# Expert input matrices laid out by halves of the input, with a stationary router and rearranged additions behind the experts

## The reference

```
h2  = modulate(x, norm2_g, sh2, sc2)                  # 256 x 1024
gp  = softmax(h2 @ w_rg + b_rg)                       # 4 groups
el  = h2 @ w_re + b_re                                # 32 experts, 8 a group
g   = top1(gp); e0, e1 = top2(softmax(el[g]))         # two experts for each token
moe = sum over the two: weight * ((silu(h2 @ w1[e]) * (h2 @ w3[e])) @ w2[e])
x   = x + g2 * moe
x   = rms_norm(x, norm_f_g)                           # then the second block's own norm, and q, k, v
```

## Time and profile before

| | |
|---|---|
| median of 3 runs | 1377.7 us (1375.81 to 1378.25) |
| the profiled execution's own time | 1377.22 us |
| its span | 1375.4 us |
| mean granted TensorE clock | 0.944 |
| busy: PE, DVE, ACT | 1153.6, 611.5, 540.8 us |
| HBM read | 394.97 MB |
| chain that ended last | PE 61%, DMA 20%, DVE 10%, ACT 7%, issue 2% |
| loads of expert matrices | 52 into the five extra slots, 44 into the ring |

### The profile page before, as it was taken

How to read it: one execution, slowest core, us unless ns; L and a number is a source line. 1 busy time by engine, 2 the same in 40 slices (tenths; PEclk the granted TensorE clock), 3 DMA queues, 4 the chain that set the end, 5 groups by cost and what they waited for, 6 DMA issues and landing times.

```text
span 1375.4 us, 22370 instructions
## 1 busy us (share of the span) xinstructions
PE 1153.6 (84%) x9627; PEld 917.0 (67%) x9627; DVE 611.5 (44%) x1363; ACT 540.8 (39%) x1203; POOL 0.2 (0%) x4
## 2 busy tenths in 40 slices
PE   6989998857475666657589989999999989999997
PEld 4867678534243443424257757999998758899997
DVE  4564664201110110101165765665555855655554
ACT  4554553211101111101155665555554654655553
POOL 0000000000000000000000000000000000000000
PEclk9999998989788889978899999999999999999999
DMA  9895847899999999999978655555546655655520
GB/s 390 345 356 223 355 186 294 341 427 427 428 426 426 424 427 427 426 426 428 426 299 307 235 194 198 231 184 184 185 153 230 228 215 184 245 184 184 184 93 31
DMA packets 29569, 397.53 MB, mean 289 GB/s; under 512 B 3480, under 2 KB 4888, under 8 KB 5400
## 3 DMA queue, kind: packets, MB, share of 16 engines
q1 hardware_dynamic: 29032, 395.72, 72.1%
q10 hardware_dynamic: 432, 0.30, 0.1%
HBM read 394.97 MB, written 1.05 MB: 288 GB/s over the span
## 4 chain that ended last, share of the span: by engine, by line
PE 61%; DMA 20%; DVE 10%; ACT 7%; issue 2%; SPq 0%; ACTq 0%; DVEq 0%
PE ps L141 61%; DMA mem<-in_w 13%; DMA ring<-in_w 5%; DVE mem L141 5%; DVE memr L141 3%; ACT mem L141 3%; ACT memr L141 3%; DMA ring<-in_wpk 1%; DVE small L141 1%; DMA posi<-in_pos 1%; ACT L141 0%; ACT rowb L141 0%; DVE x L141 0%; SPq L141 0%; DVE mcol L141 0%
## 5 line engine op out<-in xcount | busy, mean ns | idle before, releaser
L141 PE MATMUL ps<-memr 128*128 128x256 f32 (+1 forms) x4680 | 670.6, 303 | 17.9 <-DVE memr L141 17.9
L141 PEld LDWEIGHTS ps<-memr 128*128 128x128 f32 x4680 | 612.4, 193 | 62.5 <-DVE memr L141 27.8
L141 DVE TENSOR_TENSOR memr<-ring,memr 128x512 fp32r<-128x512 f32 x440 | 297.7, 690 | 247.0 <-ACT memr L141 243.6
L141 PE MATMUL ps<-mem 128*32 128x256 f32 (+5 forms) x2360 | 299.1, 421 | 86.8 <-DMA ring<-in_w 34.9
L141 ACT ACTIVATE memr<-ring 128x512 fp32r<-128x512 f32 x440 | 268.2, 627 | 221.6 <-PE ps L141 214.6
L141 PEld LDWEIGHTS ps<-mem 128*32 128x32 f32 (+3 forms) x2360 | 185.9, 150 | 158.6 <-issue 106.7
L141 ACT ACTIVATE mem<-ps 128x256 f32<-128x256 f32 (+5 forms) x307 | 121.3, 407 | 417.4 <-PE ps L141 415.4
L141 PE MATMUL ps<-ring,mem 128*32 128x256 f32 x1408 | 150.4, 428 | 40.5 <-DMA mem<-in_w 35.7
L141 DVE TENSOR_TENSOR mem<-mem,ps 128x256 f32<-128x256 f32 (+1 forms) x76 | 31.7, 418 | 270.3 <-ACT mem L141 270.3
L141 PEld LDWEIGHTS ps<-ring,mem 128*32 128x32 f32 x1408 | 72.8, 122 | 78.9 <-issue 53.3
L141 DVE COPY mem<-ps 32x256 f32<-32x256 f32 (+2 forms) x81 | 38.2, 471 | 118.7 <-PE ps L141 117.7
(11 more groups left out here) (91 smaller groups left out, 379.7 us busy)
## 6 DMA issues: line engine op xcount, KB each, us to landing
ring<-in_wpk SPq DMA_DIRECT2D x89, 2048.0 KB, 8.1
mem<-in_w SPq DMA_DIRECT2D x52, 2048.0 KB, 34.4
ring<-in_w SPq DMA_DIRECT2D x44, 2048.0 KB, 36.5
mem<-in_wpk SPq DMA_DIRECT2D x1, 2048.0 KB, 10.4
ring<-in_wpk SPq DMA_DIRECT2D x2, 1024.0 KB, 5.3
x<-in_x SPq DMA_DIRECT2D x2, 512.0 KB, 5.7
out_dram<-mem SPq DMA_DIRECT2D x4, 256.0 KB, 2.2
cst<-in_cst SPq DMA_DIRECT2D x1, 944.0 KB
```

The costliest lines, as they stand in the source:

```text
L141: ins = o[1](*o[2], **o[3])
```

## The change

The host packs `w1` and `w3` of an expert into two matrices of 2 MB: `w13a` holds input tiles 0 to 3 of both, `w13b` tiles 4 to 7. The 32 calls keep their order; the first 16 wait for `w13a` alone, and release it. The last unit of the experts (w2 of expert 31) is loaded as two halves by separate DMAs, the second half issued first. The router weights become the stationary operand: eight calls with 256 moving columns give 40 x 256 logits, which DVE copies to `lgT` and PE transposes back in two parts, behind the first four transposes of `hT`. Behind the experts each addition waits for its own bank, the first four squares no longer wait for the whole scatter, and two weight splits are issued behind the fifth square.

```diff
@@ the order of the units @@
-            for name in ("w1", "w3", "w2"):
+            for name in ("w13a", "w13b", "w2"):
@@ load_unit @@
             state["load"] += 1
-            state["recs"][n] = S.dma(ringsem[slot], slots[slot][:, 0:units[n].shape[1]], units[n], after=after)
+            w = units[n].shape[1]
+            if n == moe_last - 1:
+                w = w // 2
+                last_half.append(S.dma(s_half, slots[slot][:, w:2 * w], units[n][:, w:2 * w], after=after))
+                after = []
+            state["recs"][n] = S.dma(ringsem[slot], slots[slot][:, 0:w], units[n][:, 0:w], after=after)
@@ router @@
-            for tt in range(2):
-                r = mm(ps[:, 40 * tt:40 * tt + 40], hT[:, k, 128 * tt:128 * tt + 128], w40[:, k, :], k == 0 and tt == 0,
-                       k == 7 and tt == 1, after=fr + [h_r[k], ld_rows])
-        lg_r = V(vt.tensor_tensor, lg, ps[:, 0:80].rearrange("p (t n) -> p t n", t=2),
-                 bc(rows[:, R_BR:R_BR + 40], [128, 2, 40], 1), ALU.add, after=[r, ld_rows])
-        PB.give(b, [lg_r])
+            r = mm(ps[0:40, 0:256], w40[:, k, :], hT[:, k, :], k == 0, k == 7, after=fr + [h_r[k], ld_rows])
+        lgT = sq[0:40, 0, :]
+        lgT_r = V(vt.tensor_copy, lgT, ps[0:40, 0:256], after=[r] + sq_free[0])
+        PB.give(b, [lgT_r])
+        lg_r = None
...
+                if lg_r is None:
+                    b, ps, fr = PB.take()
+                    for t_ in range(2):
+                        r = T(te.transpose, ps[:, 40 * t_:40 * t_ + 40], lgT[:, 128 * t_:128 * t_ + 128],
+                              cst[0:40, K_ID:K_ID + 40], after=fr + [lgT_r])
+                    lg_r = V(vt.tensor_tensor, lg, ps[:, 0:80].rearrange("p (t n) -> p t n", t=2),
+                             bc(rows[:, R_BR:R_BR + 40], [128, 2, 40], 1), ALU.add, after=[r, ld_rows])
+                    PB.give(b, [lg_r])
@@ group @@
-                for k in range(8):
-                    for j in range(4):
-                        w = (w1u, w3u)[j // 2]
-                        r = mm(ps[32 * j:32 * j + 32, 0:256], xgT[:, k, 32 * q:32 * q + 32],
-                               w[:, k, 256 * (j % 2):256 * (j % 2) + 256], k == 0, k == 7, after=fr + [l1, l3, xgr[g][k]])
-                release(r)
-                release(r)
+                for half in range(2):
+                    w13, ld = unit("rows")
+                    for k in range(4 * half, 4 * half + 4):
+                        for j in range(4):
+                            r = mm(ps[32 * j:32 * j + 32, 0:256], xgT[:, k, 32 * q:32 * q + 32],
+                                   w13[:, k % 4, 256 * j:256 * j + 256], k == 0, k == 7, after=fr + [ld, xgr[g][k]])
+                    release(r)
...
-                               w2u[:, kx, 256 * j:256 * j + 256], kx == 0, kx == 3, after=fr + [a, l2])
+                               w2u[:, kx, 256 * j:256 * j + 256], kx == 0, kx == 3,
+                               after=fr + [a, l2] + (last_half if e == 31 and kx >= 2 else []))
@@ additions behind the experts @@
-                        after=[acc_r[3], ada_rec[(0, 10 + n // 4)]])
+                        after=[acc_r[n // 2], ada_rec[(0, 10 + n // 4)]])
             if n % 2:
                 PB.give(a_[0], [x1_r[n]])
-            sq_r[n] = A(sc.activation, sqX[:, n, :], xT[:, n, :], ACT.Square, after=[x1_r[n]] + moe_r)
+            sq_r[n] = A(sc.activation, sqX[:, n, :], xT[:, n, :], ACT.Square,
+                        after=[x1_r[n]] + (moe_r if n >= 4 else []))
+            if n == 4:
+                st["hold"] = False
+                stage(2)
+                st["hold"] = True
@@ host @@
+def tile_both(a, b):
+    return np.stack([a.reshape(8, 128, 512), b.reshape(8, 128, 512)], 2).transpose(1, 0, 2, 3).reshape(128, -1)
...
-        "w1": np.stack([tile_rows(w) for w in i["w1"][0]]), "w3": np.stack([tile_rows(w) for w in i["w3"][0]]),
+        "w13a": np.stack([tile_both(a, b)[:, 0:4096] for a, b in zip(i["w1"][0], i["w3"][0])]),
+        "w13b": np.stack([tile_both(a, b)[:, 4096:8192] for a, b in zip(i["w1"][0], i["w3"][0])]),
```

More of the change, by code:

```diff
@@ L288, in program @@
             mem[:, WB + o:WB + o + UNIT] for o in (4096, 14360, 10264)]
+        s_half, last_half = sem("s_half"), []
         def load_unit(slot, after):
@@ L1187, in program @@
                 PB.give(b, [xr[-1]])
-        hT_last = r
+                hT_last = r
+                if lg_r is None:
[6 more added lines that the diff above has]
+                    PB.give(b, [lg_r])
         load_unit(RING + 4, [hT_last])
@@ L1386, in group @@
                 e = 4 * g + q
-                w1u, l1 = unit("cols")
-                w3u, l3 = unit("cols")
                 b, ps, fr = PB.take()
-                for k in range(8):
-                    for j in range(4):
-                        w = (w1u, w3u)[j // 2]
-                        r = mm(ps[32 * j:32 * j + 32, 0:256], xgT[:, k, 32 * q:32 * q + 32],
-                               w[:, k, 256 * (j % 2):256 * (j % 2) + 256], k == 0, k == 7, after=fr + [l1, l3, xgr[g][k]])
-                release(r)
-                release(r)
+                for half in range(2):
[5 more added lines that the diff above has]
+                    release(r)
                 xgT_free[0] = [r]
@@ L1495, in program @@
                 nst = 0
[L1496 to L1508, removed]
+                for k in range(8):
+                    ld = Rec(s_ext, 16, True)
+                    S.wait(hx_free)
+                    S.cur.append(("op", dyn_load, (nc, t, "w13a" if k < 4 else "w13b", k % 4, ereg, w8), {}, ld))
+                    for j in range(4):
+                        r = mm(ps[32 * j:32 * j + 32, 0:256], xgT[:, k, 32 * q:32 * q + 32],
+                               w8[:, 256 * j:256 * j + 256], k == 0, k == 7, after=fr + [ld] + gr)
+                    hx_free = [r]
                 xgT_free[0] = [r]
```

## The result

Twenty runs of each kernel: 1379.8 us before, 1376.9 us after, in the medians. The ratio is 0.9977, with a 95% interval of 0.9967 to 0.9988. The change is faster by about 3 us, where I had forecast 5.9, and 1376.9 lies outside my range. Two things are mixed in that miss. The median of before moved up 2.1 us between the first three runs and the twenty, which an absolute number can't follow. And half of the gain is missing, which is the subject of the rest.

The account below looks back on a forecast made before the run. The expert stage was taken as bound by its load stream at about 427 GB/s, so only its start and surroundings count. 1.8 + 0.4 + 2.3 + 1.4 = 5.9 us off 1377.7 gave 1371.8 us, range 1369.0 to 1375.3.

Parts of the forecast that it names:

- First release: Start of the expert stream: w13a released after 16 calls lets the tenth unit be issued earlier, 1.8 us gained.
- a start that is 1 us earlier is an end that is 1 us earlier: Expert load stream: continuous once the tenth unit lands, so an earlier start moves its end by the same amount.
- Rival D: Stream start: not earlier, because the slowest DMA queue still has work; loses up to 2.2 us, 1374, chance 0.06.
- Router: Router ahead of expert 0: 256-column matmuls bring the bias 0.4 us earlier, bounds 0.8 earlier and 2.6 later.
- Tail: Last expert: only half the first layer follows w13b's landing, so w2 ends 2.3 us earlier, ends 1.2 and 3.1.
- Additions: Behind the experts: additions start during the scatter and two splits move forward, 1.4 us earlier, ends 0 and 2.8.
- Split of the last unit: Expert 31's w2 load in halves: worth nothing, as the first calls wait for the half issued second.
- rival E: Last unit: its first half does help, w2's first calls starting early; 1 us more, 1370.8, chance 0.03.
- Rival A: Last expert: shorter bursts between waits leave w2 and part of the scatter at 1.2 GHz; gain about 3 us, 1374.7, chance 0.22.
- Rival C: Additions: the moved splits wait for the first unit behind the experts; price 1 to 2 us, 1373.3, chance 0.05.
- Rival B: Last expert: clock stays at 1.2 GHz through w2, scatter and sums of squares; slower than before, 1380.4, chance 0.04.
- Behind 707.71 everything keeps its distances and is limited by PE and its slots, so nothing is given back: From slab 4 to the end: distances stay the same, so the whole upstream gain reaches the end.

Follow-up runs that it names:

- e1: The changed kernel again, with nothing altered, for a second profile; ratio 0.9990 to the kernel before.
- e3: The kernel before with only the w13a and w13b layout (old router, last unit whole, old additions); ratio 0.9976 to before.
- e2: The changed kernel with the router of before put back; ratio 0.9991 to the kernel before.
- g3: The changed kernel with the old router and PE's waits at router, tail and late place filled with unused matmuls; ratio 0.9931 to before.
- h2: The changed kernel with PE's waits at the router and the late place (97 to 103 us behind slab 4) filled with unused matmuls; ratio 0.9934 to before.
- e4: The kernel before with only the additions for each bank and the two splits between them; ratio 0.9991 to before.
- f5: The kernel before with only the waits ahead of expert 31's first layer and the last scatter filled with unused matmuls; ratio 0.9993 to before.
- i1: The plain changed kernel again, beside one with the late place filled; ratio 0.9973 to the kernel before.
- f1: The changed kernel with PE's waits at router and tail, not the late place, filled with unused matmuls; ratio 0.9946 to before.
- f4: The changed kernel with PE's waits at router, tail and late place all filled with unused matmuls; ratio 0.9946 to before.

## Why the prediction was wrong

**The mechanism up to slab 4 was right, and nearly the size.** Against the router's first matmul, slab 4 came 5.5 us earlier in two of three profiles of the changed kernel, and 1.1 in the first, with router and w2 at 1.2 GHz; I had summed 5.9. In e1 the parts are 1.6 at the tenth issue (20.8 to 19.2, halves and router together, where I had 2.2), 2.9 at the tail and 1.1 at the additions.

- *First release, 1.8 us.* Tenth issue 18.9 us behind the router's first matmul in e3 against 20.8: 1.9. And "a start that is 1 us earlier is an end that is 1 us earlier" held: from the tenth issue to the last landing it is 434.4 us before (681.25 - 246.87) and 434.4 and 434.5 in two profiles of the changed kernel (680.67 - 246.24 in e1, 683.76 - 249.28 in the first). Rival D is out.
- *Router, 0.4 us, bounds 0.8 earlier and 2.6 later.* Both cases occur: 3.65 and 6.61 us of matmuls, tenth issue 19.2 and 22.3. I had argued that the fall would not come there because the matmuls are larger; in the first profile it had come before they began, in PE's wait (granted 0.60 from 226 to 227), and stayed to their end. In time the new router is worth nothing, either way, beside the old one (e2, g3).
- *Tail, 2.3 us, ends 1.2 and 3.1.* From the last landing to the end of w2: 5.2 us before, 2.2 in e1, 3.6 in the first profile. The gain is 2.9 or 1.6, within the ends, and the term stands.
- *Additions, 1.4 us.* 16.4 us became 15.3, in every kernel that has them. The term was 0.3 us too large.
- *Split of the last unit, nothing.* As forecast, so rival E did not occur; turned round it brings the 0.8 us of one pair of profiles.
- *Rival A, a cold tail, 0.22,* is what the first profile shows, and its 3 us of gain is what the medians gave. But filling the tail, alone beside the late place, gave nothing, so as far as these runs show it had the right time for another reason. The Trainium skill's advice to do all tiles of the contraction ahead of the next wait (TensorE: Matmul & The Clock Gate, oscillation) is given because waits for loads put PE back to the low clock. The traces agree in part: in the first profile, e3 and h2 w2 ran at that clock, 3.44, 3.64 and 3.64 us instead of 1.93, and in e1 it ran at 2.4 GHz, although PE had waited 2.97 us for w13b and done that half's matmuls at the low clock (3.52 us). Rival C did not occur: the two subtractions follow their copies without a wait for a load. Rival B did not occur.

**The step that failed** is the sentence "Behind 707.71 everything keeps its distances and is limited by PE and its slots, so nothing is given back". The distances changed: 669.2 to 669.8 us from slab 4 to the end instead of 667.7 in the profile of before, and of 665.6 in e4. The clock fell some 99 us behind slab 4 in all five profiles that have all three parts (halves, split, additions) and no filling there, and in none of the four that have fewer (before, e3, e4, f5). Filling that place is worth 2 us to the changed kernel within one group and 4 across groups, and nothing measurable to before. With it filled in both, the pair stands at 0.9951 (the mean of three) and 0.9994, 6 us apart, about my sum. This pairing crosses groups, so the agreement may be luck; the pairs with everything filled within a single group gave 4.3 and 4.8. So the sentence was wrong, and what it left out is a loss of the size of the missing 3 us; that nothing else took part is not shown.

**What stays open.** Why the fall finds the changed kernel and misses the other is not shown. The instructions at that place are the same, and so are the two waits ahead of the fall (0.78 and 0.71 us in i1, 0.76 and 0.71 in before); only their moment differs. How often each execution meets the fall is known only from the mean clocks above. Why router and tail filled without the late place (f1) are worth as much as all three (f4) in one group, and beside it add something only together in another, is open too. And e2 at 0.9991 lies above e3 at 0.9976 though it has more parts. The late fall in its profile (669.6 against 668.6) explains 1 us of that 2, and e2's executions had the lowest mean granted clock of all the eighteen kernels, 0.9409 against e3's 0.9428.

**The version to keep** is the changed one with all three places filled: 0.9946 and 0.9911 in two groups, 0.9927 with the halves turned round, that is 7 to 12 us under before and 4 to 9 under the change.

## What to carry to other kernels

In a kernel that is bound by PE behind a bound transfer stream, a gain upstream shifts all that follows against the changes of the matmul clock, and a few microseconds can be taken or given far from the edit: after the milestones of the edit, compare the distance from the last of them to the end. Take two or three profiles of a kernel before reading a difference of 0.3% out of one, judge such differences by fixed distances, not spans, and look up where the profiled execution stands among the others. If PE has waits of about 1 us in a row on its critical stretch, matmuls on constants in them are cheap to try; try them in the kernel before too, or their gain is booked to the change.

## What the runs showed of the hardware

The clock fell in a stretch in which PE never waited over 1.1 us at a time: waits of 0.78 and 0.71 us from 797 to 800 in i1, the fall near 800.3 (an estimate from the 0.54 of 800 to 804), and 1.02 us behind it. I had looked for falls behind waits of 2 us and more only. In i1 PE still worked 2.98 of 4 us in the slice where it fell. In before it worked 2.17 and 2.38 of 4 us at that place, with waits of 0.76, 0.71, 0.54 and 1.47 us, and the clock stayed at 2.4 GHz.

The tenth unit, issued together with the eleventh before (0.37 us apart), landed 8.8 us later; issued alone it took 7.7 and 7.8 (the changed kernel, e1). The unit behind it landed 5.8 and 5.6 us later rather than 4.9, so this gave nothing in the end: only the moment of the issue counted.
